# Starting each weight tile without waiting for every PSUM pair, and interleaving two tiles behind each norm

## The reference: two layers of a hybrid trunk on 640 tokens

```python
def swiglu(h, w1, w2):
    gate, up = jnp.split(h @ w1, 2, axis=-1)
    return (jax.nn.silu(gate) * up) @ w2

# one layer
h = rms_norm(x, norm_g[l, 0]) * (1 + sc1) + sh1
x = x + 0.5 * gt1 * swiglu(h, ffn_w1[l, 0], ffn_w2[l, 0])     # w1 1024 x 5632, w2 2816 x 1024
h = rms_norm(x, norm_g[l, 1]) * (1 + sc2) + sh2
p = h @ w_in                                                   # then two mixers on p
x = x + gt2 * (mixers(p) @ w_out)
h = rms_norm(x, norm_g[l, 2]) * (1 + sc3) + sh3
x = x + 0.5 * gt3 * swiglu(h, ffn_w1[l, 1], ffn_w2[l, 1])
```

## Time and profile before

| | |
|---|---|
| median of 3 runs | 3564.59 us (3561.26 to 3566.76) |
| time of the profiled execution | 3561.52 us |
| its span, first to last instruction | 3559.6 us |
| PE busy | 3152.2 us, 89% |
| DVE busy | 1508.1 us, 42% |
| ACT busy | 974.0 us, 27% |
| mean granted clock of TensorE, share of full speed | 0.920 |
| matmuls of `linear`, six groups of 1944 on h and six of 704 on g | 15888 |
| transfers | 264.86 MB, mean 74 GB/s |

### The profile page before, as it was taken

One profiled execution on the slowest core, in us unless ns is written; L12 is line 12 of the kernel. 1 busy time (PEld: TensorE's weight loads), 2 busy tenths in 40 slices (PEclk: granted clock), 3 DMA queues, 4 the chain that ended last, 5 costly groups with the idle time before them and its releaser, 6 DMA issues.

```text
span 3559.6 us, 60193 instructions
## 1 busy us (share of the span) xinstructions
PE 3152.2 (89%) x25821; PEld 2964.3 (83%) x25821; DVE 1508.1 (42%) x2068; ACT 974.0 (27%) x1301; POOL 212.1 (6%) x293
## 2 busy tenths in 40 slices
PE   6999998888677778999998999998986798899998
PEld 4999997768566767999997999997885668899998
DVE  3655643335445544655655522223234343322222
ACT  3321213223222223321213321213344353331221
POOL 0000000000333200000000000000010000000000
PEclk9999999879688879999999999999978899999999
DMA  5443432010000012443432332211001002121221
GB/s 205 149 136 119 148 113 72 18 54 30 5 5 3 3 60 65 148 137 119 149 124 83 113 99 66 79 64 53 30 13 37 9 1 77 53 80 63 71 78 46
DMA packets 68051, 264.86 MB, mean 74 GB/s; under 512 B 7776, under 2 KB 7904, under 8 KB 67456
## 3 DMA queue, kind: packets, MB, share of 16 engines
q1 hardware_dynamic: 47808, 184.72, 16.0%
q0 software_dynamic: 20032, 76.98, 6.8%
HBM read 257.87 MB, written 3.81 MB: 74 GB/s over the span
## 4 chain that ended last, share of the span: by engine, by line
PE 84%; DVE 8%; ACT 4%; issue 2%; DMA 1%; POOL 0%; SPq 0%; DVEq 0%; ACTq 0%; POOLq 0%
PE ps L1819 33%; PE ps L1820 33%; PE ps L1676 1%; DVE normed L2156 1%; DVE h_lo L2143 1%; PE ps L1882 1%; PE ps L1883 1%; PE ps L850 1%; PE ps L856 1%; PE ps L1656 1%; PE ps L1362 1%; PE ps L866 1%; DMA ring<-w_ada 1%; PE ps L1664 1%; PE ps L546 1%
## 5 line engine op out<-in xcount | busy, mean ns | idle before, releaser
L335 DVE TENSOR_TENSOR w_lo<-ring,w_hi 128x1024 fp32r<-128x1024 f32 (+1 forms) x307 | 401.5, 1309 | 1335.8 <-ACT w_hi L330 1334.6
L330 ACT ACTIVATE w_hi<-ring 128x1024 fp32r<-128x1024 f32 (+1 forms) x307 | 345.6, 1126 | 1567.9 <-PE ps L1820 1353.1
L1819 PE MATMUL ps<-h_hi,w_hi 128*128 128x320 f32 x1944 | 616.9, 317 | 122.6 <-DVE h_lo L2143 58.0
L1820 PE MATMUL ps<-h_lo,w_hi 128*128 128x320 f32 x1944 | 607.5, 312 | 0.0
L1819 PE MATMUL ps<-h_lo,w_hi 128*128 128x320 f32 x1944 | 607.4, 312 | 0.0
L1819 PE MATMUL ps<-h_hi,w_lo 128*128 128x320 f32 x1944 | 607.2, 312 | 0.0
L1820 PE MATMUL ps<-h_hi,w_hi 128*128 128x320 f32 x1944 | 607.2, 312 | 0.0
L1820 PE MATMUL ps<-h_hi,w_lo 128*128 128x320 f32 x1944 | 606.6, 312 | 0.0
L1819 PEld LDWEIGHTS ps<-h_hi,w_hi 128*128 128x128 f32 x1944 | 370.7, 191 | 143.8 <-issue 69.1
L1820 PEld LDWEIGHTS ps<-h_hi,w_hi 128*128 128x128 f32 x1944 | 371.5, 191 | 0.0
L1819 PEld LDWEIGHTS ps<-h_hi,w_lo 128*128 128x128 f32 x1944 | 371.1, 191 | 0.0
(11 more groups left out here) (347 smaller groups left out, 4001.0 us busy)
## 6 DMA issues: line engine op xcount, KB each, us to landing
late_mem<-w_ada POOLq DMA_DIRECT2D x128, 512.0 KB, 3.8
ring<-w_up0a SPq DMA_DIRECT2D x44, 512.0 KB, 3.6
ring<-w_up0b SPq DMA_DIRECT2D x44, 512.0 KB, 3.5
ring<-w_up1a SPq DMA_DIRECT2D x44, 512.0 KB, 3.5
ring<-w_up1b SPq DMA_DIRECT2D x44, 512.0 KB, 3.5
ring<-w_down0a SPq DMA_DIRECT2D x16, 704.0 KB, 4.0
ring<-w_down0b SPq DMA_DIRECT2D x16, 704.0 KB, 4.1
ring<-w_down1a SPq DMA_DIRECT2D x16, 704.0 KB, 4.0
```

The lines of the kernel that those rows point to most:

```text
L330: act.activation(w_hi[:, n % SPLITS, 0:cols], ring[:, r, 0:cols], ACT.Copy).then_inc(high_ready, 1)
L335: dve.tensor_tensor(w_lo[:, n % SPLITS, 0:cols], ring[:, r, 0:cols], w_hi[:, n % SPLITS, 0:cols].bitcast(F32), ALU.subtract).then_inc(spli ...
L1819: pe.matmul(left, weights, acts[:, k, LEFT], start=start, stop=stop)
L1820: mm = pe.matmul(right, weights, acts[:, k, RIGHT], start=start, stop=stop)
```

## The change

Feed-forward stages no longer call `pairs_read`. Wherever `ready` is given (the `up` half a behind norm0 and norm2, `ret` and `mlstm` behind norm1, and `out` behind the mixers), a new function `first_two` runs tiles 0 and 1 block by block: block k of tile 0, then block k-3 of tile 1. The tiles from 2 on follow one by one, written out. `ready` is no longer given to half b of `up`, and the tiles 4, 8, ... no longer wait on it.

```diff
@@ -37,6 +37,7 @@
+BEHIND = 3
@@ -1798,31 +1799,56 @@
                 b0, n0 = blk0[layer, name], tile0[layer, name]
-                pairs_read(layer, name)
+                if name not in STEPS:
+                    pairs_read(layer, name)
                 reader, f0 = (free_act, free0[layer, name]["act"]) if name in PROJECTIONS else \
                              (free_dve, free0[layer, name]["dve"])
 
-                def one(i, u):
+                def begin(i, u):
+                    pe.wait_ge(reader, i * 4 + f0 + u + 1 - SETS)
+                    pe.wait_ge(split_ready, i * 4 + RING + n0 + u + 1)
+
+                def block(u, k):
                     left, right, _ = pair((b0 + u) % SETS)
                     s = (n0 + u) % SPLITS
-                    pe.wait_ge(reader, i * 4 + f0 + u + 1 - SETS)
-                    pe.wait_ge(split_ready, i * 4 + RING + n0 + u + 1)
+                    w_h, w_l = w_hi[:, s, k * P:(k + 1) * P], w_lo[:, s, k * P:(k + 1) * P]
+                    first, last = k == 0, k == k_blocks - 1
+                    for weights, acts in ((w_h, hi), (w_h, lo), (w_l, hi)):
+                        start, stop = first and weights is w_h and acts is hi, last and weights is w_l
+                        pe.matmul(left, weights, acts[:, k, LEFT], start=start, stop=stop)
+                        mm = pe.matmul(right, weights, acts[:, k, RIGHT], start=start, stop=stop)
+                    return mm
+
+                def one(i, u):
+                    begin(i, u)
                     for k in range(k_blocks):
-                        if ready is not None and u == 0:
-                            pe.wait_ge(ready[0], ready[1] + k + 1)
                         if last_k is not None and k == k_blocks - 1:
                             pe.wait_ge(gated_ready, last_k)
-                        w_h, w_l = w_hi[:, s, k * P:(k + 1) * P], w_lo[:, s, k * P:(k + 1) * P]
...
+                        mm = block(u, k)
...
-                if name in STEPS and (layer, int(name[-2])) in MD_FIRST:
+                def first_two():
+                    for k in range(k_blocks + BEHIND):
+                        if k < k_blocks:
+                            if k == 0:
+                                begin(0, 0)
+                            pe.wait_ge(ready[0], ready[1] + k + 1)
+                            mm = block(0, k)
+                            if k == k_blocks - 1:
+                                mm.then_inc(tiles_done, 1)
+                        if k >= BEHIND:
+                            if k == BEHIND:
+                                begin(0, 1)
+                            mm = block(1, k - BEHIND)
+                    mm.then_inc(tiles_done, 1)
+
+                if ready is not None:
+                    first_two()
+                    for t in range(2, n):
+                        one(t // 4, t % 4)
+                elif name in STEPS and (layer, int(name[-2])) in MD_FIRST:
                     for t in range(n):
                         one(t // 4, t % 4)
                 else:
@@ -1896,7 +1922,8 @@
                         for half in "ab":
-                            linear(layer, f"up{j // 2}{half}", 2 * HALF_F, DB, h_hi, h_lo, ready=ready)
+                            linear(layer, f"up{j // 2}{half}", 2 * HALF_F, DB, h_hi, h_lo,
+                                   ready=ready if half == "a" else None)
```

More of the change, by code:

```diff
@@ L1810, in one @@
+                def one(i, u):
+                    begin(i, u)
                     for k in range(k_blocks):
-                        if ready is not None and u == 0:
-                            pe.wait_ge(ready[0], ready[1] + k + 1)
                         if last_k is not None and k == k_blocks - 1:
                             pe.wait_ge(gated_ready, last_k)
-                        w_h, w_l = w_hi[:, s, k * P:(k + 1) * P], w_lo[:, s, k * P:(k + 1) * P]
-                        first, last = k == 0, k == k_blocks - 1
```

## The result

The changed kernel takes 3449.0 us (median of four runs, 3446.9 to 3463.6) against 3562.9 before: ratio 0.9693, 95% interval 0.967 to 0.9717, or 3.1% faster. I had forecast 3467 and a range of 3459 to 3486.

What follows compares the result with a forecast made beforehand. The prediction took PE, busy for 3152 of 3560 us, as the bound. From the profiled 3561.52 us it took 57.6 + 22.3 + 18.0 = 97.9, giving 3463.6, then added 3.07 for 3467 us; range 3459 to 3486.

Steps and rivals of the forecast that it cites:

- Joins of up and down: Eight joins from up to down: PE's wait and the half-clock matmuls after it both go, 57.6 us.
- tile 0's room for g: Down's tile 0 needs g's last block only in its last k, with 2.95 us to spare.
- Joins of down and up b: Four joins from down to the second half of up: the wait for the last tile's residual goes, 22.3 us.
- Norms: Six stretches behind norms, from tile 0 to tile 2: interleaving tile 1 into tile 0's waits wins 18.0 us.
- The stall for tile 2's split: Behind a norm in the four up stages: a new wait for `w_lo` of about 0.5 us before tile 2.
- the rival that the interleaving loses the clock: Behind the norms the clock falls, interleaving wins between nothing and half; 3476 to 3485 us, chance 0.15.
- The warning that the prediction took for it: Behind the norms: an engine idling a little between matmul groups keeps falling to slow clock; norms win about nothing, total about 80 us.
- `out`: Stage behind the mixers, also given `first_two`: h is complete before its weights, so 0, half a us each way.
- Written-out tiles: 68 tiles formerly in loops: forecast worth 0 at 7.04 us a tile; the slower rival had chance 0.02.
- the 97.9 of the sum: Total us forecast to be won at both kinds of join and behind the norms: 57.6 + 22.3 + 18.0.
- the bounds of the norm part (21 and 0): Behind the norms: at most 21 us with no stall, at least nothing if PE runs at half clock.
- the last term of the sum: Whole kernel: 3.07 us added because the median shown lay that far above the profiled execution.

Runs made afterwards that it cites:

- e12: Changed kernel with five unread matmuls filling the pauses before the retention outputs, and ACT's loop of the up half behind a norm written out; median 3445.8 us.
- e11: Changed kernel with four extra VectorE products ahead of the first weighting of retention scores, lengthening PE's pause; 3466.2 to 3473.7 us.
- e4: The changed kernel profiled again, with no edit; ratio to before 0.9685, runs 3447.3 to 3464.8 us.
- e8: Changed kernel with one extra VectorE product on scratch, meant to delay retention by 0.7 us; runs 3448.8 to 3466.6 us.
- e15: Changed kernel with all joins, but tiles 0 and 1 interleaved only behind norm1 of layer 0; nothing filled; runs 3459.2 to 3482.9 us.
- e1: Kernel before with only the wait for all pairs dropped in the feed-forward stages; ratio to before 0.9765.
- e7: Kernel before with four extra VectorE products on scratch after retention's rotations, delaying the output stretch by 2.45 us; runs 3563.3 to 3568.7 us.
- e16: Changed kernel without the interleaving behind norm1 of layer 0 only; nothing filled; runs 3467.4 to 3473.7 us.
- e2: Changed kernel with the wait for all pairs put back, leaving only the interleaved tiles; ratio to before 0.9958.
- e3: The kernel before profiled again, with no edit; runs 3557.0 to 3566.3 us.
- e6: Kernel before with one extra VectorE product on scratch after retention's rotations, meant to delay it by 0.7 us; runs 3550.9 to 3569.2 us.
- e10: Kernel before with five unread matmuls filling PE's pauses ahead of the retention outputs; runs 3543.8 to 3553.6 us.

## Why the prediction was right and where it was wrong

**Joins of up and down:** forecast 57.6, trace 57.4 us. Both halves went, the wait and the slow matmuls behind it, and tile 0's room for g held: 2.9 us against 2.95 forecast. **Joins of down and up b:** forecast 22.3, trace 22.3. **Norms:** forecast 18.0, trace 17.3. The windows are 18.66 for up (18.5 forecast) and 18.02 for `ret` and `mlstm` (17.95). The stall for tile 2's split is where it was forecast, and e12 shows that its cause is the table load. The clock rises once at the start of each interleaved stretch and does not fall again in it, so the rival that the interleaving loses the clock did not come true. The warning that the prediction took for it from the Trainium skill (TensorE: Matmul & The Clock Gate, A second HAM failure mode: psum-queue depth-cycling) is thus not borne out in this place. The Trainium skill's same page, HAM oscillation — how this bites in real kernels, says that a matmul engine which waits long enough between groups (there for a DMA) drops to the slow clock and starts the next group at it; the joins before (5.0 us of waiting, then 0.53) and e11 (a pause of 3.2 us, then 0.50) agree. The prediction's own reason, that PE at 89% is near the 1.00 of ordinary tiles, is no safe guide, though: the trace before has the retention outputs at 98% busy and a clock of 0.51. **`out`:** forecast 0 with half a us each way; its two stretches went from 32.9 to 31.9, by the clock at their start. **Written-out tiles** take 7.04 us, no slower. The kernels with the stretch pinned agree in runs: 99.8 us against the 97.9 of the sum.

**What failed** is the step from the sum to the time, "the bounds of the norm part (21 and 0) and the runs' own scatter of 5 us" as all that the range has to hold. The sum took the mixers as fixed, a term of 0 without a reason beyond their unchanged code. The traces show that they are not fixed: the retention output stretch takes 40.1 or 23.3 us for the same instructions, by whether the clock falls in its first microseconds. That is worth 16.8 us; a lower end that takes it in is 3459 - 17 = 3442, and it holds the measured 3449. The whole gap of 17.7 us between forecast and median has two parts. The profiled execution became 110.8 us shorter and not 97.9: retention gave 19.1, the start, `out`, the norms themselves and small rests 4.0, the other mixers took 9.4 back and the windows 0.9. The other 4.8 are the last term of the sum, the median at 3.07 above the profiled execution: behind the change the median lies 1.7 below it. So the size of the gap is in part chance, and the stretch alone would have been more than enough to leave the range. The row that held the warning was the clock in the page and in the windows of retention (0.66 with PE busy for 70%); I read only `linear`. The three runs shown lay within 6 us and looked like a stable kernel; it was one in which the clock nearly always falls in that stretch.

**Still open:** why the two parts together let the clock stay up in most runs. It isn't the length of the pauses (1.59 and 1.17 against 1.57 and 1.18 us), and both traces enter retention with the same instructions. One thing differs: how long before the stretch the clock last rose. In the eleven profiles in which neither pause was filled or lengthened (the first is 1.3 to 1.6 us there, the second 1.2), it is 5.4 to 5.75 us in the four that stayed at full clock (after, e4, e8, e15), and 5.0 to 5.2 (e1, e7, e16) or 5.95 to 5.97 (before, e2, e3, e6) in the seven that fell, 1.7 to 1.9 or 0.9 us into the stretch. That speaks for theory D, that the moment of the pauses decides, but no run set this distance on purpose, so it is not shown. The other mixers vary too, RWKV between 441.3 and 451.2 us over the kernels profiled here and attention between 174.0 and 177.1; no run tells what decides those.

## What to carry to other kernels

Count a wait at a join twice: once for the idle time and once for the matmuls at half clock behind it (here 5.0 and 1.6 us at the join of the earlier trace rows). When the time of an untouched stage hangs on the clock that it is granted, say so and widen the range by what it takes at the one clock and at the other, since an edit ahead of it can go with the other one. Before calling a small kernel change good or bad by some 15 us, pin such a stretch, for instance with a few matmuls nobody reads; 10 us of scatter can still be left (e10, e12). And look in the trace whether a delay that was put in delays anything: those of e6 and e8 did not.

## What the hardware showed that I had not expected

A stretch in which PE was busy for 98% of the time stayed at 0.50 from 0.9 us after its start to its end, 39 us on (before), while dense tiles of 128 x 320 matmuls came back to 1.00 within 3.7 us. These are 128- and 64-row float32 matmuls of 128 columns. Where the clock did not fall in its first two us, the same stretch kept 1.00 (to its end, or to its last 0.2 us in most kernels with fillers). I had taken a low clock for something that only the first few microseconds after a pause pay. What keeps it low here no run tells.
